# Third attention written out unit by unit, with the products of query tiles two to seven set between its units

## The chip, the cores and the metric

One core of one Trainium2 chip runs the program. The metric is the time of one execution on the device in microseconds (us); of several runs the median counts. Six names are used: PE does the matrix products (PEld is its loading of weights, meaning the stationary operand), DVE, ACT and POOL are the vector, scalar and GpSimd engines, and SP issues most transfers from HBM. Each engine works through its own queue in order, and engines wait for each other on counting semaphores.

## The reference, cut to what matters

The program is a two-block network of 512 tokens and width 1024. Nearly all of it is large products in split precision; the change touches only the last attention, a sliding-window one with sinks, and the projections just before it:

```python
h = rms_norm(x, ln_mix_pre[1])
q, k, v = split(h @ w_in + b_in)          # 16 query heads of 64, 2 key and value heads
s = q . k * 64 ** -0.5                    # blocks of 128 queries against their own and the previous block
s = where(band, s, -inf)
mx = maximum(max(s), sink)
e = exp(s - mx)
p = e / (sum(e) + exp(sink - mx))
o = (p . v) @ w_out + b_out
```

## The kernel before

**Products.** Every 32-bit operand is held as a rounded part and a rest (`_hi`, `_lo`), and `three` (L756 to L765) makes three PE products for each block of 128 rows: hi by hi, lo by hi, hi by lo. A column tile of weights ("chunk") takes eight such steps, 24 products of 512 columns. A chunk arrives as `w_raw` by a transfer of SP, ACT rounds it (`split`, L1449), POOL makes the rest (`rest`, L618), and it stays in a ring of four until PE has used it (`chunks_used`). ACT and POOL work three chunks ahead.

**Projections before the attention.** In this order PE makes the key tile `sk`, the value tile `sv`, query tile `sq0` (in bank 2), the turn of `sv`, and then `sq1` to `sq7`, alternating between banks 0 and 1 of PSUM. For each tile DVE multiplies the bank by the norm (`scaled_by_root`, L2659) and adds bias (`biased`, L2653), ACT rounds its two heads (`round_queries`, L1564), and DVE makes their rests (`rest_of_queries`, L2124). Only then does the attention begin.

**The attention.** There are 64 units, one for each of 16 heads and four blocks of 128 queries; the first block of a head has one block of keys, the others two. A unit passes through these steps: PE makes the scores (`scores`, two products, L967); DVE masks and finds the maximum (`maximum`, L2139); ACT takes the exponential (`exponentials`, L1583); PE turns it (`transposes`, L979); ACT moves the turned tile out of the bank (`move_transposed`, L1598); PE multiplies by the values (`values`, L1008); and after each fourth unit DVE writes a head's output (`output`, L2246). POOL adds the sink's share to the sums (`add_sink`, L668). The order on PE is scores of unit n+5, transposes of n+2, values of n. Scores lie in four banks. PE reads a query head from `q_stage2`, into which POOL copies it (`stage`, L652) ahead of time. Pairs of heads are a loop, with the first pair and the last pairs unrolled.

**Behind it** eight tiles of the output are turned and split (`concat`, `turn_output`, L1055) between the products of the next chunk.

The names on which the steps rest stand in these functions:

## Time and profile before

| | us |
|---|---|
| three runs | 2467.21, 2469.01, 2470.68 (median 2469.01) |
| span of the profiled execution, first to last instruction | 2468.0 |
| PE busy in it | 2423.7 (98%) |
| ACT, POOL, DVE busy | 1079.6, 972.3, 936.0 |
| query tiles one to seven | from 1941.07 to 1979.25 |
| third attention | from 1979.25 to 2039.2 |

The profiled execution has no time of its own apart from its span, which is 1.0 us under the median. A row of the timeline gives start, duration, engine, line, operation, what is written and read, the shapes, and in brackets how long the engine had been idle and who ended that. Durations of PE's products overlap, so that their price is the distance from one start to the next. A window's row gives, for each engine, busy time and number of instructions, then the granted clock of PE (1.00 is 2.4 GHz, 0.50 is 1.2 GHz), the share of the transfer engines and GB/s.

### The profile page before, as it was taken

Reading aid. Unit: us, or ns where it says so; the run is one execution under the profiler, and the core shown is the slowest. Engines: PE = TensorE matmul, PEld = TensorE weight load, DVE = VectorE, ACT = ScalarE, POOL = GpSimd, SP = SyncE. Lnnn points to the kernel's source line nnn. Section 1 sums busy time; section 2 is a strip of 40 time slices with the busy share of each in tenths; the row PEclk is TensorE's granted clock in tenths of the full one; section 3 lists DMA queues with packets and bytes.
Section 4 is the critical chain, followed back from the end, with each engine's and each line's share of the span. In section 5 each row is a group of like instructions: output and inputs, shape, how many; then the busy total and the mean of one; then the engine's idle time right before and its main releaser. Section 6 shows DMA issues by size and latency. Waiting matters only on the chain.

```text
span 2468.0 us, 36248 instructions
## 1 busy us (share of the span) xinstructions
PE 2423.7 (98%) x11990; PEld 2004.0 (81%) x11990; DVE 936.0 (38%) x2051; ACT 1079.6 (44%) x1917; POOL 972.3 (39%) x484
## 2 busy tenths in 40 slices
PE   8999999999999999999999999999999999999998
PEld 6888888888778978888887978788888797788886
DVE  7976322211477753222214243321211773311212
ACT  7565443432347754444335534432332583432321
POOL 4821444444331124444443413444443423444441
PEclk9999999999999999999999999999999999999999
DMA  4300333333420013233332312233333202233331
GB/s 154 116 30 18 90 97 101 94 102 105 128 69 10 1 35 94 93 102 93 103 102 79 103 39 81 77 95 95 100 94 94 69 18 69 86 101 95 94 94 68
DMA packets 57866, 202.75 MB, mean 82 GB/s; under 512 B 7072, under 2 KB 7968, under 8 KB 57392
## 3 DMA queue, kind: packets, MB, share of 16 engines
q1 hardware_dynamic: 54864, 196.02, 26.2%
q10 hardware_dynamic: 2912, 5.55, 0.6%
q8 instruction: 55, 0.90, 0.1%
q14 instruction: 35, 0.29, 0.0%
HBM read 199.44 MB, written 2.10 MB: 82 GB/s over the span
## 4 chain that ended last, share of the span: by engine, by line
PE 41%; issue 14%; POOL 7%; ACT 1%; DVE 1%; POOLq 0%; DVEq 0%; ACTq 0%
PE bank L764 36%; POOL w_lo L618 7%; PE bank L1008 1%; PE bank L967 1%; PE bank L979 1%; ACT h_hi L1492 1%; PE bank L1372 0%; PE bank L1353 0%; ACT gained L1495 0%; PE bank L1367 0%; PE bank L793 0%; PE bank L1055 0%; PE bank L881 0%; PE bank L770 0%; PE bank L786 0%
## 5 line engine op out<-in xcount | busy, mean ns | idle before, releaser
L618 POOL TENSOR_TENSOR w_lo<-w_raw,w_hi 128x1024 fp32r<-128x1024 f32 x368 | 883.3, 2401 | 1197.7 <-ACT w_hi L1449 1188.1
L764 PE MATMUL bank<-h_hi,w_hi 128*128 128x512 f32 x1648 | 650.5, 395 | 7.2 <-DVE tmp L2476 2.1
L764 PE MATMUL bank<-h_lo,w_hi 128*128 128x512 f32 x1648 | 642.2, 390 | 0.0
L764 PE MATMUL bank<-h_hi,w_lo 128*128 128x512 f32 x1648 | 642.2, 390 | 0.0
L1449 ACT ACTIVATE w_hi<-w_raw 128x1024 fp32r<-128x1024 f32 x368 | 386.8, 1051 | 242.7 <-PE bank L764 214.0
L764 PEld LDWEIGHTS bank<-h_hi,w_hi 128*128 128x128 f32 x1648 | 309.8, 188 | 82.3 <-issue 5.9
L764 PEld LDWEIGHTS bank<-h_hi,w_lo 128*128 128x128 f32 x1648 | 309.7, 188 | 65.2
L764 PEld LDWEIGHTS bank<-h_lo,w_hi 128*128 128x128 f32 x1648 | 309.9, 188 | 65.0 <-issue 2.2
L764 PE MATMUL bank<-mact_hi,w_hi 128*128 128x512 f32 x512 | 199.3, 389 | 1.7 <-DVEq L2342 1.7
L764 PE MATMUL bank<-mact_hi,w_lo 128*128 128x512 f32 x512 | 199.2, 389 | 0.0
L764 PE MATMUL bank<-mact_lo,w_hi 128*128 128x512 f32 x512 | 199.2, 389 | 0.0
L764 PE MATMUL bank<-act_hi,w_hi 128*128 128x512 f32 x352 | 136.9, 389 | 0.0
L764 PE MATMUL bank<-act_lo,w_hi 128*128 128x512 f32 x352 | 136.9, 389 | 0.0
L764 PE MATMUL bank<-act_hi,w_lo 128*128 128x512 f32 x352 | 136.9, 389 | 0.0
L1583 ACT ACTIVATE tmp<-bank,nmax 128x128 f32<-128x128 f32 (+2 forms) x240 | 119.1, 496 | 19.7 <-DVE nmax L2139 12.0
L2340 DVE TENSOR_TENSOR tmp<-sq,bank 128x512 f32<-128x512 f32 x64 | 44.0, 688 | 200.2 <-ACT sq L1661 200.2
L1647 ACT ACTIVATE act_hi<-tmp 128x512 f32 x44 | 27.8, 632 | 207.6 <-DVE tmp L2327 207.6
L764 PEld LDWEIGHTS bank<-mact_hi,w_hi 128*128 128x128 f32 x512 | 96.1, 188 | 21.8 <-issue 1.8
L1598 ACT ACTIVATE sq<-bank 128x128 f32<-128x128 f32 (+3 forms) x232 | 92.7, 401 | 48.1 <-PE bank L1008 44.8
L764 PEld LDWEIGHTS bank<-mact_lo,w_hi 128*128 128x128 f32 x512 | 96.1, 188 | 19.9
L764 PEld LDWEIGHTS bank<-mact_hi,w_lo 128*128 128x128 f32 x512 | 96.1, 188 | 19.8
L979 PE MATMUL bank<-ident,tmp 128*128 128x128 f32 x548 | 107.1, 284 | 3.6 <-ACT tmp L1583 1.5
(403 smaller groups left out, 3489.3 us busy)
## 6 DMA issues: line engine op xcount, KB each, us to landing
w_raw<-in_weights SPq DMA_DIRECT2D x368, 512.0 KB, 3.6
out<-x ACTq DMA_DIRECT2D x8, 256.0 KB, 2.1
x<-in_xT SPq DMA_DIRECT2D x4, 256.0 KB, 6.8
x<-in_xT ACTq DMA_DIRECT2D x4, 256.0 KB, 7.4
memx<-in_memT SPq DMA_DIRECT2D x1, 1024.0 KB, 9.8
cmp_w1k<-in_cmp_w ACTq DMA_DIRECT2D x1, 1024.0 KB, 5.6
...
```

What stands on the lines that cost most here:

```text
L618: nc.gpsimd.tensor_tensor(w_lo[:, t % RING, :], w_raw[:, t % RAW, :], w_hi[:, t % RING, :].bitcast(F32), ALU.subtract).then_inc(lo_ready, 1)
L764: r = nc.tensor.matmul(out, a, b, start=first and n == 0, stop=last and n == 2)
L967: r = nc.tensor.matmul(out[:, 0:n], q, k, start=part == 0, stop=part == 1)
L979: r = nc.tensor.transpose(probT_bank[g % 2][:, n * P:(n + 1) * P], prob[:, g % 2, n * P:(n + 1) * P], ident[:, :])
L1008: r = nc.tensor.matmul(output_place(kind, u, g), probT[:, g % 2, n * P:(n + 1) * P], v, start=n == 0, stop=n == len(kts) - 1)
L1449: nc.scalar.activation(w_hi[:, t % RING, :], w_raw[:, t % RAW, :], ACT.Copy).then_inc(hi_ready, 1)
L1492: nc.scalar.activation(h_hi[:, k, :], x_bank(k) if k < BY_PE else x[:, k, :], ACT.Identity, scale=col(name, k)).then_inc(gain_rounded, 1)
L1583: nc.scalar.activation(prob[:, g % 2, 0:n], score_bank[bank_of(kind, u)][:, 0:n], ACT.Exp, bias=nmax[:, s4:s4 + 1], scale=1.0 if kind.star ...
L1598: nc.scalar.activation(probT[:, g % 2, 0:n], probT_bank[g % 2][:, 0:n], ACT.Copy).then_inc(probT_ready[g % 2], 1)
L1647: nc.scalar.activation(act_hi[:, bass.ds(2 * i + f, 1), :].rearrange("p a n -> p (a n)"), tmp[:, f, :], ACT.Copy).then_inc(act_rounded, 1)
L2340: nc.vector.tensor_tensor(tmp[:, f % 2, :], sq[:, f % 2, :], bank[b % 2][:, :], ALU.mult).then_inc(act_made, 1)
```

## The change

- Queries are no longer scaled by 64 ** -0.5; the keys are, once. DVE's bias step for the queries goes: ACT adds the bias while it rounds, and DVE while it makes the rest.
- `q_stage2` and POOL's copies into it go. PE reads `q_swa` itself and waits for `q_split`.
- `sq1` gets bank 3. `sq2` to `sq7` all accumulate in bank 1, one after another. Each is cut into its eight steps of three products: steps 0 to 3 of `sq2` stand before the attention, steps 4 to 7 behind the scores of units 0 to 3, and the 40 steps of `sq3` to `sq7` between transposes and values of units 0 to 39.
- The first step of each of them waits until DVE has moved the tile before it out of bank 1 (`query_moved`). DVE does so at units 0, 8, 16, 24, 32 and 40, behind the maximum of unit n+4 and the output of unit n.
- Scores use three banks (2, 3, 0), and their lead over the values goes from five units to four. The loops are written out.
- POOL makes the rests of the chunks of `sq5` to `sq7` and of the first three chunks of the output projection in four quarters each, behind the sinks of heads 0, 2, 4, 6, 8 and 10. ACT splits those chunks at units 4, 12, 20, 28, 36 and 44, and rounds the queries of tile 2+j at units 8j+1 and 8j+2.

```diff
-OWN["sq0"] = 2
+OWN.update({"sq0": 2, "sq1": 3}, **{f"sq{j}": 1 for j in range(2, KT)})
...
+LOOK_AHEAD = 4
+def swa_unit(n):
+    return (f"swa{n // 32}", 0, n % 8, n % 32 // 8) if n < 64 else None
+def query_step(s):
+    return f"sq{2 + s // KT}", s % KT
+QUERY_STEPS = (KT - 2) * KT
+EARLY_STEPS = 8
...
+    if kind.startswith("swa"):
+        return (32 * int(kind[3]) + 8 * i + u) % 3
...
+            def rest_in_quarters(t):
+                pool.wait_ge(hi_ready, t + 1)
+                for n in range(0, KT * P, 2 * P):
+                    part = slice(n, n + 2 * P)
+                    r = nc.gpsimd.tensor_tensor(w_lo[:, t % RING, part], w_raw[:, t % RAW, part], w_hi[:, t % RING, part].bitcast(F32), ALU.subtract)
+                r.then_inc(lo_ready, 1)
...
+            end = CHUNK["sq1"] + AHEAD + 1
+            rests(start, end)
+            for head in range(2 * SWA_PAIRS):
+                add_sink(*swa_unit(TT * head))
+                if head in (0, 2, 4, 6, 8, 10):
+                    rest_in_quarters(end)
+                    end += 1
+            start = norms(end, ["mlppre1"])
...
+                if kind.startswith("swa") and u % TT == 0:
+                    pe.wait_ge(q_split, 24 + heads_before(kind, u) + 2 * i + 1)
...
-                    pe.wait_ge(probs_ready, g - kind.startswith(("dsa", "mem0", "swa")) + per * i)
+                    pe.wait_ge(probs_ready, g - kind.startswith(("dsa", "mem0")) + per * i)
...
-                    for j in range(1, KT):
-                        column_tile(f"sq{j}")
-                    wait_evacuated(pe, "svT")
-                    pe.wait_ge(first_query_moved, 1)
+                    t = CHUNK["sq1"]
+                    chunk_ready(t)
+                    for k in range(KT):
+                        r = three(of("sq1")[:, :], slot(t, k), (h_hi[:, k, :], h_lo[:, k, :]), k == 0, k == KT - 1)
+                    r.then_inc(chunks_used, 1)
+                    def query_products(s):
+                        name, k = query_step(s)
+                        if k == 0:
+                            chunk_ready(CHUNK[name])
+                            pe.wait_ge(query_moved, int(name[2]) if s else 1)
+                        r = three(of(name)[:, :], slot(CHUNK[name], k), (h_hi[:, k, :], h_lo[:, k, :]), k == 0, k == KT - 1)
+                        if k == KT - 1:
+                            r.then_inc(chunks_used, 1)
+                    for name in ("sk", "sv", "svT"):
+                        wait_evacuated(pe, name)
+                    for s in range(4):
+                        query_products(s)
                     pe.wait_ge(k_split, 13)
-                    def banks_free():
-                        for j in (KT - 2, KT - 1):
-                            wait_evacuated(pe, f"sq{j}")
-                    attention_stream(pe, STREAMS[2], lambda at: attention_begin(at, banks_free), pair_of_heads)
+                    for n in range(4):
+                        if n < 2:
+                            pe.wait_ge(query_moved, n + 1)
+                        scores(*swa_unit(n))
+                        query_products(4 + n)
+                    for n in range(2):
+                        transposes(*swa_unit(n))
+                    for n in range(2 * 4 * SWA_PAIRS):
+                        if swa_unit(n + LOOK_AHEAD):
+                            scores(*swa_unit(n + LOOK_AHEAD))
+                        if swa_unit(n + 2):
+                            transposes(*swa_unit(n + 2))
+                        if EARLY_STEPS + n < QUERY_STEPS:
+                            query_products(EARLY_STEPS + n)
+                        values(*swa_unit(n))
...
+                    def round_query(j, heads=(0, 1)):
+                        act.wait_ge(query_moved, j + 1)
+                        for hh, (part, hi, _) in enumerate(both_heads("swa0", j, sq_q[:, j, :])):
+                            if hh in heads:
+                                bias = col("swa_b_q", j)[HD * hh:HD * hh + HD, :]
+                                nc.scalar.activation(hi, part, ACT.Identity, bias=bias).then_inc(q_rounded, 1)
+                    round_query(0)
+                    split_ahead(CHUNK["sq1"])
+                    round_query(1)
+                    for n in range(LOOK_AHEAD - 1):
+                        exponentials(*swa_unit(n))
+                    for n in range(2):
+                        move_transposed(*swa_unit(n))
+                    for n in range(2 * 4 * SWA_PAIRS):
+                        if swa_unit(n + LOOK_AHEAD - 1):
+                            exponentials(*swa_unit(n + LOOK_AHEAD - 1))
+                        if swa_unit(n + 2):
+                            move_transposed(*swa_unit(n + 2))
+                        done = 2 + n // 8
+                        if n % 8 in (1, 2) and done < KT:
+                            round_query(done, [n % 8 - 1])
+                        if n % 8 == 4 and done < KT:
+                            split_ahead(CHUNK[f"sq{done}"])
...
+                    def move_query(j):
+                        wait_product(dve, f"sq{j}")
+                        nc.vector.tensor_tensor(sq_q[:, j, :], of(f"sq{j}")[:, :], rstd_late[:, :], ALU.mult).then_inc(query_moved, 1)
+                    def rest_of_query(j, heads=(0, 1)):
+                        dve.wait_ge(query_moved, j + 1)
+                        for hh, (part, hi, lo) in enumerate(both_heads("swa0", j, sq_q[:, j, :])):
+                            if hh in heads:
+                                dve.wait_ge(q_rounded, 24 + 2 * j + hh + 1)
+                                bias = col("swa_b_q", j)[HD * hh:HD * hh + HD, :]
+                                nc.vector.scalar_tensor_tensor(lo, part, bias, hi.bitcast(F32), ALU.add, ALU.subtract).then_inc(q_split, 1)
+                    scaled_by_root("sk", sk[:, :])
+                    biased(0, sk[:, :], col("swa_bk"), SCALE)
+                    scaled_by_root("sv", diag[:, :])
+                    biased(1, diag[:, :], col("swa_bv"))
+                    move_query(0)
                     rest_of_both(9, sk[:, :], *k_swa)
-                    last = KT - 1
-                    for j in range(last):
-                        projected(f"sq{j}", j + 2, sq_q[:, j, :], col("swa_b_q", j), SCALE)
-                        if j:
-                            rest_of_queries("swa0", j - 1, sq_q[:, j - 1, :])
-                    scaled_by_root(f"sq{last}", sq_q[:, last, :])
-                    def pair_between_rests(per, at):
-                        for u in range(per):
-                            unit_of_pair(u, at)
-                            if u == 0:
-                                biased(last + 2, sq_q[:, last, :], col("swa_b_q", last), SCALE)
-                            elif u in (1, 2):
-                                rest_of_queries("swa0", last - 1, sq_q[:, last - 1, :], [u - 1])
-                            elif u in (5, 6):
-                                rest_of_queries("swa0", last, sq_q[:, last, :], [u - 5])
-                    attention_stream(dve, STREAMS[2], attention_begin, pair_of_heads, pair_between_rests)
+                    rest_of_query(0)
+                    move_query(1)
+                    hold_sink(0, 0)
+                    for n in range(LOOK_AHEAD):
+                        maximum(*swa_unit(n))
+                    rest_of_query(1)
+                    for n in range(2 * 4 * SWA_PAIRS):
+                        if swa_unit(n + LOOK_AHEAD):
+                            maximum(*swa_unit(n + LOOK_AHEAD))
+                        output(*swa_unit(n))
+                        done = 2 + n // 8
+                        if n % 8 == 0 and done < KT:
+                            move_query(done)
+                        if n % 8 in (2, 3) and done < KT:
+                            rest_of_query(done, [n % 8 - 2])
```

On PE, where the third attention begins, before:

```order
L967 MATMUL bank<-k_swa_hi,q_stage 128x256 [waits probs_ready,evacuated1,evacuated0]
L967 MATMUL bank<-k_swa_lo,q_stage 128x256
L967 MATMUL bank<-k_swa_hi,q_stage 128x256 [waits probs_ready]
L967 MATMUL bank<-k_swa_lo,q_stage 128x256
L770 MATMUL bank<-masks_b,ident_b 128x384 x2
L979 MATMUL bank<-ident,tmp 128x128 [waits probT_ready0,probs_ready]
L967 MATMUL bank<-k_swa_hi,q_stage 128x128 [waits probs_ready,q_staged]
L967 MATMUL bank<-k_swa_lo,q_stage 128x128
L979 MATMUL bank<-ident,tmp 128x128 [waits probT_ready1,probs_ready]
L979 MATMUL bank<-ident,tmp 128x128
```

and in the changed kernel, from the transposes of unit 0 (L1003 are transposes, L991 scores, L783 the products of query tiles, L1032 values):

```order
L1003 MATMUL bank<-ident,tmp 128x128 [waits probT_ready0,probs_ready]
L1003 MATMUL bank<-ident,tmp 128x128 [waits probT_ready1,probs_ready]
L1003 MATMUL bank<-ident,tmp 128x128
L991 MATMUL bank<-k_swa_hi,q_swa 128x128 [waits probs_ready,q_split]
L991 MATMUL bank<-k_swa_lo,q_swa 128x128
L1003 MATMUL bank<-ident,tmp 128x128 [waits probT_ready0,probs_ready]
L1003 MATMUL bank<-ident,tmp 128x128
L783 MATMUL bank<-h_hi,w_hi 128x512 [waits query_moved,lo_ready]
L783 MATMUL bank<-h_lo,w_hi 128x512
L783 MATMUL bank<-h_hi,w_lo 128x512
L1032 MATMUL bank<-sv,sq 128x64 [waits o_done,probT_ready0]
```

The filler products are gone, the query products stand between transposes and values, and the first of them waits for `query_moved`.

On DVE, around the last query tiles of before (L2659 moves a tile, L2653 adds bias, L2124 makes rests, L2139 is the maximum):

```order
L2659 TENSOR_TENSOR sq_q<-bank,spare 128x512 [waits chunks_used]
L2653 TENSOR_SCALAR sq_q<-sq_q,cols 128x512 [waits evacuated0]
L2124 TENSOR_TENSOR q_swa<-sq_q,q_swa 64x512 [waits q_rounded,swa_biased]
L2124 TENSOR_TENSOR q_swa<-sq_q,q_swa 64x512
L2659 TENSOR_TENSOR sq_q<-bank,spare 128x512 [waits chunks_used]
L2143 COPY sink_now<-nsinks 128x1 [waits evacuated1]
L2139 ISA bank,nmax<-bank,masks_b,sink_now 128x128 [waits scores_ready,sink_held]
L2139 ISA nmax 128x1
```

and around unit 8 of the changed kernel, where tile `sq3` is moved (L2304 is the output of a head, L2197 the maximum, L2721 the move):

```order
L2197 ISA bank,nmax<-bank,masks_b,sink_now 128x256 [waits scores_ready]
L2197 ISA nmax 128x1
L2201 COPY sink_now<-nsinks 128x1
L2231 TENSOR_SCALAR sink_shift<-nmax,sinks 128x4 [waits max_ready]
L2304 TENSOR_TENSOR o_tok<-bank,rinv 128x4x64 [waits pv_done,rinv_ready]
L2197 ISA bank,nmax<-bank,masks_b,sink_now 128x128 [waits scores_ready,sink_held]
L2197 ISA nmax 128x1
L2721 TENSOR_TENSOR sq_q<-bank,spare 128x512 [waits chunks_used]
L2197 ISA bank,nmax<-bank,masks_b,sink_now 128x256 [waits scores_ready]
```

The move of a tile used to follow only work on other tiles; now it stands behind a head's output, which waits for `pv_done`, and behind a maximum, which waits for `scores_ready`.

On POOL, in the attention of before (L668 adds the sink, L652 copies a head):

```order
L214 COMPARE_AND_BRANCH
L668 TENSOR_TENSOR oscale<-psum_p,sinkexp 128x4 [waits sink_ready]
L652 COPY q_stage<-q_swa 128x512 [waits q_staged,scores_ready,q_split]
L668 TENSOR_TENSOR oscale<-psum_p,sinkexp 128x4 [waits sink_ready]
L652 COPY q_stage<-q_swa 128x512 [waits q_staged,scores_ready,q_split]
```

and in the changed kernel (L685 adds the sink, L635 is a quarter of a rest, L627 a whole one):

```order
L685 TENSOR_TENSOR oscale<-psum_p,sinkexp 128x4 [waits sink_ready]
L635 TENSOR_TENSOR w_lo<-w_raw,w_hi 128x256 [waits hi_ready]
L635 TENSOR_TENSOR w_lo<-w_raw,w_hi 128x256 x3
L685 TENSOR_TENSOR oscale<-psum_p,sinkexp 128x4 [waits sink_ready] x2
L635 TENSOR_TENSOR w_lo<-w_raw,w_hi 128x256 [waits hi_ready]
```

The copies are gone, and each odd head's sink but the last two now stands behind the rest of a chunk, which waits for `hi_ready`.

## Rows read from the trace of the kernel before

**Rows 1.** Windows: engines' busy time and the granted clock (PEclk) by stage.

```profile
1941.07:1979.25 38.18, 38.18 (x172) 31.63 (x171) 29.82 (x30) 19.11 (x26) 19.60 (x10) 1.00 0.32 98
1979.25:1984.50 5.25, 3.61 (x25) 2.66 (x24) 4.16 (x17) 3.48 (x13) 2.63 (x3) 1.00 0.32 100
1984.50:1991.40 6.90, 6.90 (x36) 6.90 (x35) 4.70 (x16) 5.24 (x19) 0.88 (x3) 0.51 0.00 1
1991.40:2035.00 43.60, 43.55 (x387) 43.24 (x386) 35.59 (x161) 41.46 (x173) 9.83 (x25) 1.00 0.00 1
2039.20:2042.60 3.40, 3.33 (x17) 3.34 (x17) 1.39 (x3) 1.67 (x3) 0.00 (x0) 0.51 0.00 0
```

**Rows 2.** Timeline of PE where the third attention begins; brackets: idle before, and releaser.

```profile
1979.25 0.22 PE L967 MATMUL bank<-k_swa_hi,q_stage 128*128 128x128 f32 x1
...
1980.24 0.35 PE L967 MATMUL bank<-k_swa_hi,q_stage 128*128 128x256 f32 x1 [0.37 <-issue]
...
1980.79 0.50 PE L770 MATMUL bank<-masks_b,ident_b 128*128 128x384 bf16 x2
1981.56 0.33 PE L979 MATMUL bank<-ident,tmp 128*128 128x128 f32 x1 [0.28 <-ACT tmp L1583]
...
1982.33 0.44 PE L979 MATMUL bank<-ident,tmp 128*128 128x128 f32 x2 [0.26 <-ACT tmp L1583]
...
1983.75 0.44 PE L979 MATMUL bank<-ident,tmp 128*128 128x128 f32 x2 [0.73 <-ACT sq L1598]
```

**Rows 3.** Timeline of PE in four units of the settled attention.

```profile
1999.04 0.31 PE L967 MATMUL bank<-k_swa_hi,q_stage 128*128 128x128 f32 x1
...
2000.58 0.36 PE L967 MATMUL bank<-k_swa_hi,q_stage 128*128 128x256 f32 x1
...
2000.90 0.38 PE L979 MATMUL bank<-ident,tmp 128*128 128x128 f32 x2
2001.12 0.56 PE L1008 MATMUL bank<-sv,sq 128*128 128x64 f32 x4
...
2002.28 0.31 PE L967 MATMUL bank<-k_swa_hi,q_stage 128*128 128x128 f32 x1
```

**Rows 4.** Timeline of PE in concat, transposes (L1055) between products (L764).

```profile
2043.70 0.48 PE L764 MATMUL bank<-h_hi,w_hi 128*128 128x512 f32 x1
...
2044.49 0.60 PE L1055 MATMUL bank<-ident,o_tok 128*128 128x128 f32 x4
2044.84 0.48 PE L764 MATMUL bank<-h_hi,w_hi 128*128 128x512 f32 x1
```

**Rows 5.** Timeline of ACT before and at the attention's start.

```profile
1941.94 1.06 ACT L1449 ACTIVATE w_hi<-w_raw 128x1024 fp32r<-128x1024 f32 x1
1942.90 0.58 ACT L1466 ACTIVATE sv<-bank 128x512 f32<-128x512 f32 x1
1948.22 1.29 ACT L1564 ACTIVATE q_swa<-sq_q 64x512 fp32r<-64x512 f32 x2 [4.74 <-DVE sq_q L2653]
...
1978.65 1.28 ACT L1583 ACT_TABLE_LOAD   x1
1981.05 0.37 ACT L1583 ACTIVATE tmp<-bank,nmax 128x128 f32<-128x128 f32 x1 [1.12 <-DVE nmax L2139]
```

**Rows 6.** DVE: one tile's instructions (minimum/median/maximum ns), before the attention.

```profile
L2134 DVE TENSOR_TENSOR k_swa_lo<-sk,k_swa_hi x4: 683/686/2773, 1942.0 to 1946.2; 64x512 fp32r<-64x512 f32 x4
```

**Rows 7.** Timeline of DVE: a tile moved, and a maximum.

```profile
1979.44 0.69 DVE L2659 TENSOR_TENSOR sq_q<-bank,spare 128x512 f32<-128x512 f32 x1 [1.18 <-PE bank L764]
...
1980.51 0.36 DVE L2139 CUSTOM_DVE_ANT_0 bank<-bank,masks_b,sink_now 128x128 f32<-128x128 f32 x1 [0.18 <-DVE sink_now L2143]
```

**Rows 8.** Timeline of DVE: a head's output, in the settled attention.

```profile
2009.99 0.43 DVE L2246 TENSOR_TENSOR o_tok<-bank,rinv 128x256 f32<-128x256 f32 x1
```

**Rows 9.** Timeline of POOL: the rest of a chunk, and a sink.

```profile
1943.08 2.59 POOL L618 TENSOR_TENSOR w_lo<-w_raw,w_hi 128x1024 fp32r<-128x1024 f32 x1 [5.16 <-ACT w_hi L1449]
...
1983.60 0.20 POOL L668 TENSOR_TENSOR oscale<-psum_p,sinkexp 128x4 f32<-128x4 f32 x1 [2.51 <-ACT sinkexp L1589]
```

85 lines of the change are left out of this document (25 added, 60 removed).

## The prediction

> **What bounds the kernel now.** I read the page first: PE is busy 98% of the span, so only what PE executes or waits for counts. Then I read windows over the part that the change touches. From 1941.07 to 1979.25 PE makes query tiles one to seven without a gap: 7 x 24 = 168 products in 38.18 us, 0.227 us each [rows 1]. From 1979.25 to 1984.50 it is busy for only 3.61 of 5.25 us, while it waits for the first exponentials and their copies [rows 1, 2]. Then it is busy all the time but at 1.2 GHz for 6.90 us, and from 1991.40 to 2035 it is busy for 43.55 of 43.60 us at 2.4 GHz [rows 1]. In that settled stretch four units take 1999.04 to 2002.28, that is 3.24 us or 0.81 a unit [rows 3]. ACT is busy for 41.46 of those 43.60 us, so it has 5% to spare and is the next bound there [rows 1]. So there are two things to win: the idle start, and the slow clock behind it. PE is full before and after them, and whatever makes it wait there is new time.
>
> **What goes.** Idle before PE at the start is 0.37 + 0.28 + 0.26 + 0.73 = 1.64 us, and the two filler products add (0.50 - 0.16) = 0.34 [rows 2]: 2.0 us. The slow stretch loses half of 6.9 us, 3.4 us [rows 1]. POOL's copies, DVE's bias steps and the longer scores lead all lie beside PE's work, so removing them is worth nothing in itself. The 168 products and 64 units remain.
>
> **The new start (+1.9).** PE ends `sq1` at about 1946.6 as before and four steps of `sq2` at 1949.3. Meanwhile ACT, no longer held by the roundings, splits the next chunk at once behind the move of `sv` and two roundings: 1943.5 + 1.3 + 1.06 = 1945.9 [rows 5]. POOL's rest of it then runs from 1946.0 to 1948.5 [rows 9]. The fourth rest of the keys would start on DVE at 1946.25, but such an instruction takes 0.69 us alone and took 2.77 us beside a POOL rest, ending with it [rows 6, 9]. So it ends at 1948.7, the two rests of query 0 follow at 0.69 each (taken as those of the keys), and the move of `sq1` ends at 1950.9 [rows 6, 7]. ACT rounds query 1 until 1952.25 (1.29), loads its table until 1953.5 (1.28) and has the first exponential at 1953.9 [rows 5]. The scores of unit 3 need that, since they take the first of only three banks: PE waits 0.25 + 0.5 + 1.0 us before units 0, 1 and 3. Four steps (0.68 each) and the scores (0.25 to 0.32 each) lie between. The second transposes wait 0.45 us more, because exponential 2 needs the buffer of unit 0, which is turned only at 1955.0. Then `sq3` waits for the move of `sq2`, which on DVE stands behind the two rests of query 1 and maximum 4: 1955.3 + 1.4 + 0.4 + 0.7 + 0.14 (below), at 1957.9, where PE is ready at about 1956.3. In all 3.9 us against 2.0: **+1.9**. Bounds: 0, if the start is as idle as now, and +3.
>
> The Trainium skill's page "SBUF — State Buffer", section "Who interferes with whom", says that whichever of DVE and GpSimd comes first holds their shared ports for the whole instruction and the other blocks. The 2.77 us agrees. If the two only shared the port, the start would come out about 1 us better than I have it.
>
> **The clock at the start (-1.7).** Now the clock fell behind a stretch with 1.64 of 5.25 us idle and small products otherwise, and stayed low for 6.9 us [rows 1, 2]. The new start has more idle time from 1953 to 1958, so it should fall again; but behind it come products of 512 columns, and in concat, where such products stand between transposes, the low clock lasted 3.4 us [rows 1, 4]. I take 3.4 us at half speed, which costs 1.7 instead of 3.4: **-1.7**. Ends: -3.4 (it never falls) and 0.
>
> **The wait at each new query tile (+5.8).** `sq4` to `sq7` begin at units 8, 16, 24 and 32, in the bank that the tile before them has just filled. Take the start of the scores of unit n+4 as zero. PE is ready for the new tile after those scores (0.25) and the transposes (0.22), at 0.47. On DVE the move stands behind the output of unit n-1, which waits for the values that PE issued just before zero; in the settled attention that output starts about 0.34 us after the next scores do and takes 0.43 [rows 8]. The maximum of unit n+4 follows: 0.36 us and its small read, until 1.12 [rows 7]. The move takes 0.69, until 1.81 [rows 7], and PE starts 0.14 us after what it waits for (exponential done at 1981.05 + 0.37, transposes at 1981.56) [rows 2, 5]. That is 1.95 - 0.47 = 1.48 us; I take 1.45, and 4 x 1.45 = **+5.8**. Nothing covers it, for PE is in order and the values of unit n stand behind the waiting product. The lower bound has DVE with nothing ahead of the move: 0.69 + 0.14 - 0.47 = 0.36 each, +1.4. The upper one adds 0.25 each, +6.8.
>
> **The switches (+1.0).** In concat three products and four transposes take 2043.70 to 2044.84, 1.14 us [rows 4]. Apart they would be 3 x 0.227 + 4 x 0.11 = 1.12 [rows 1, 3]. 48 such switches at 0.02 make **+1.0**; the bounds are 0 and +3.
>
> **The dense end (+2.7).** From unit 40 there are no query products left, a unit is 0.81 us again and ACT has 5% to spare. Two things fall there. First, ACT rounds query 7 at units 41 and 42 (1.29 us) [rows 5]; about half of it was lead, 0.7 us remains. Second, at unit 44 ACT splits a chunk, POOL makes its rest and only then adds the sink of head 11, for which DVE's output of unit 46 waits; behind that stands maximum 51. Counted from PE's unit 44: ACT's copy done at 1.15, split 2.2, rest 4.7, sink 5.0 [rows 5, 9], then DVE's maximum 5.7 and the exponential 6.4, where PE wants the transposes of unit 51 at 5 x 0.81 + 0.3 = 4.4. That is 2.0 us. Together **+2.7**. Bounds: 0, if the lead of the other engines takes it up, and +4.5, if the scores' shorter lead adds some or the clock falls for 3.4 us behind such a gap. The same chain at units 4 to 36 has PE steps of 0.81 + 0.68 = 1.5 us around it, and the maximum is then in time.
>
> **Sum.** +1.9 - 1.7 + 5.8 + 1.0 + 2.7 = +9.7 us on the span of 2468.0, 2477.7; the median stands 1.0 above that span, so 2478.7.
>
> **Rivals.**
>
> *Not slower: the clock stays whole.* The interleaved products of 512 columns are what PE lacked, so the clock never falls, neither at the start (-3.4) nor in concat, where now 3.4 us are at 1.2 GHz (-1.7) [rows 1], and the dense end finds its engines ahead (0). With start +1.9, tiles +5.8 and switches +1.0 this is +3.6: 2472.6, within 0.2%. For it: the falls follow idle time amid small products. Against: the new start is idler. It needs, at both places, a PE gap of 1 to 2 us leaves the clock alone as long as wide products stand on both sides of it.
>
> *Short waits.* DVE is ahead and only the move itself counts: tiles 4 x 0.36 = 1.4, start +0.5, clock -3.4, switches +1.0, end +0.7: +0.2, 2469.2. With switches at nothing and concat at full clock it is -2.5, and only past that would it be faster by 0.2%. Against: two instructions ahead of the move wait for PE's own latest work.
>
> *The clock falls at every tile.* Each gap of 1.45 us lies beside small products; if it costs 3.4 us at half speed each time, 4 x 1.7, and once more in the dense end, +8.5: 2487.2. Against: half of PE's work around the gaps is wide products, and the clock held through dense small ones [rows 1]. The Trainium skill, page "TensorE: Matmul & The Clock Gate", section "A second HAM failure mode: psum-queue depth-cycling", has a kernel whose short idles between groups of products made the clock swing; it speaks for this case, and no row here shows it.
>
> **Numbers.** The forecast gets 0.50 (own range 2474 to 2483), the whole clock 0.22, short waits 0.13, the clock falling at every tile 0.15. This measurement can tell about 0.2%, 4.9 us, from no change: below 2464.1 or above 2473.9. Faster 0.06 (the far end of short waits), same 0.30, slower 0.64. The range 2468 to 2486 leaves out the far end of short waits and most of the last rival.
>
> **What would show it.** In the timeline of PE: gaps of 1.3 to 1.6 us before the first product of `sq4` to `sq7`, ended by DVE's move, and one of some 1.6 before `sq3`; gaps of 0.5 to 1 us before the scores of units 1 and 3. Per eight units and their 24 products about 8 x 1.5 + 1.45 = 13.5 us. One window at 1.2 GHz near the start. A gap of 1 to 2 us near unit 49, ended by ACT, with POOL's sink late. I am wrong if the gaps at the tiles are under 0.8 us, or if the table load and rounding don't hold the first exponential.

## The result and the profile of the changed kernel

The changed kernel takes 2484.43 us (median of 5 runs, 2482.99 to 2485.73). The kernel before, run beside it, takes 2467.21 (5 runs, 2464.96 to 2470.68). The ratio is 1.0069, 95% interval 1.0057 to 1.0081: slower by 17.2 us. The forecast was 2478.7, in a range of 2468 to 2486: the direction held, and the size came out 5.7 us short.

The profiled execution spans 2481.2 us, 13.2 more than that of before. All of the loss lies in the attention. From the turn of `sv` to the first transposes of concat it takes 1937.78 to 2052.50, 114.7 us; before it took 1940.68 to 2039.27, 98.6. Behind that both need the same 428.7 us. Ahead of it the execution of before was 2.9 us later, since it had two stretches at 1.2 GHz in earlier parts of the program which that of after doesn't have. So +16.1 us are to be explained here, and besides them a granted clock that varies from one execution to the next.

Windows of the changed kernel (PEclk, the granted clock, is 1.00 at 2.4 GHz and 0.50 at 1.2 GHz); columns: stretch, length, busy time of PE, PEld, DVE, ACT and POOL (with counts), granted clock, DMA share, GB/s. They answer to [rows 1].

```profile
1947.00:1956.00 9.00, 5.53 (x28) 3.97 (x29) 6.13 (x18) 5.19 (x14) 0.20 (x1) 1.00 0.14 53
1956.00:1960.30 4.30, 4.30 (x19) 3.88 (x20) 0.55 (x2) 0.97 (x4) 0.00 (x0) 0.60 0.00 0
1960.30:2013.80 53.50, 47.54 (x311) 41.90 (x310) 29.68 (x106) 34.24 (x113) 12.68 (x24) 1.00 0.12 36
2013.80:2018.60 4.80, 4.74 (x20) 4.32 (x21) 0.55 (x2) 1.34 (x5) 0.00 (x0) 0.64 0.12 47
2018.60:2027.00 8.40, 8.40 (x56) 7.43 (x55) 4.86 (x16) 6.49 (x21) 2.81 (x5) 1.00 0.00 0
2027.00:2048.00 21.00, 17.81 (x144) 16.15 (x142) 14.81 (x64) 17.24 (x66) 3.90 (x11) 1.00 0.17 52
```

PE waits in three places: the start (1947 to 1956), the interleaved part (6 us idle of 53.5) and the dense end (2027 to 2048). No other engine is full in any of them: the order of the work makes PE wait, not the speed of another engine. Who ends the waits, over the whole attention (engine, line, waited for: us in total, times, longest):

```profile
PE bank L783 <- DVE sq_q L2721: 7.5, 5, 1.5
PE bank L1003 <- ACT tmp L1630: 3.1, 4, 1.5
PE bank L991 <- ACT tmp L1630: 1.1, 1, 1.1
PE bank L1077 <- DVE o_tok L2304: 0.6, 1, 0.6
PE bank L1003 <- ACT sq L1645: 0.6, 1, 0.6
PE bank L991 <- DVE q_swa L2730: 0.5, 1, 0.5
```

L783 is a query product, L991 the scores, L1003 the transposes, L1077 the first transposes of concat. The first row is the wait for a moved tile, five times 1.5 us.

**The start.** Timeline of PE, its waits (start, duration, what, and in brackets the idle time and its releaser); they answer to [rows 2]:

```profile
1947.09 0.30 PE L991 MATMUL bank<-k_swa_hi,q_swa 128*128 128x128 f32 x1 [0.51 <-DVE q_swa L2730]
1951.67 0.39 PE L991 MATMUL bank<-k_swa_hi,q_swa 128*128 128x256 f32 x1 [1.14 <-ACT tmp L1630]
1953.95 0.41 PE L1003 MATMUL bank<-ident,tmp 128*128 128x128 f32 x2 [0.58 <-ACT sq L1645]
1955.88 0.47 PE L783 MATMUL bank<-h_hi,w_hi 128*128 128x512 f32 x1 [1.51 <-DVE sq_q L2721]
```

One more, 0.15 us before the scores of unit 1 at 1948.39, is too short for the view to list.

**A new tile** (`sq4` here; `sq5` to `sq7` look the same, at 1985.65, 1999.75 and 2013.86). Timeline of POOL, DVE and PE:

```profile
1966.22 2.81 POOL L635 TENSOR_TENSOR w_lo<-w_raw,w_hi 128x256 fp32r<-128x256 f32 x4 [11.31 <-ACT w_hi L1496]
...
1968.99 0.20 POOL L685 TENSOR_TENSOR oscale<-psum_p,sinkexp 128x4 f32<-128x4 f32 x1
...
1969.22 0.18 DVE L2300 RECIPROCAL rinv<-oscale 128x4 f32<-128x4 f32 x1 [1.87 <-POOL oscale L685]
...
1970.11 0.42 DVE L2304 TENSOR_TENSOR o_tok<-bank,rinv 128x256 f32<-128x256 f32 x1
...
1970.44 0.35 DVE L2197 CUSTOM_DVE_ANT_0 bank<-bank,masks_b,sink_now 128x128 f32<-128x128 f32 x1
...
1970.71 0.69 DVE L2721 TENSOR_TENSOR sq_q<-bank,spare 128x512 f32<-128x512 f32 x1
...
1971.54 0.47 PE L783 MATMUL bank<-h_hi,w_hi 128*128 128x512 f32 x1 [1.50 <-DVE sq_q L2721]
```

Read it from the bottom. PE waits for the move; the move stands behind a maximum and a head's output; and ahead of these DVE itself had stood for 1.87 us, since POOL adds the odd head's sink only behind four quarters of a chunk's rest. The prediction had seen the first half of this and not the second.

**The dense end**, at unit 51; timeline of POOL, DVE, ACT and PE:

```profile
2034.59 2.79 POOL L635 TENSOR_TENSOR w_lo<-w_raw,w_hi 128x256 fp32r<-128x256 f32 x4 [5.71 <-ACT w_hi L1496]
...
2037.57 0.18 DVE L2300 RECIPROCAL rinv<-oscale 128x4 f32<-128x4 f32 x1 [2.49 <-POOL oscale L685]
...
2038.32 0.47 ACT L1630 ACTIVATE tmp<-bank,nmax 128x256 f32<-128x256 f32 x1 [1.30 <-DVE nmax L2197]
...
2038.94 0.33 PE L1003 MATMUL bank<-ident,tmp 128*128 128x128 f32 x1 [1.47 <-ACT tmp L1630]
```

**The ledger** of the attention, after less before:

| part | read from | us |
|---|---|---|
| start | 3.9 us of waits against 2.0 (1.64 of waits and 0.34 of filler products) | +1.9 |
| four new tiles | 4 x 1.50 | +6.0 |
| interleaving | 40 units, 74.4 us from the scores of unit 4 to those of unit 44, less 8.1 idle and 3.4 for two slow stretches, leaves 62.9; the parts alone are 40 x (0.811 + 3 x 0.2273) = 59.7 | +3.2 |
| dense end | scores of unit 44 to those of unit 60: 17.69 against four times 3.24 | +4.7 |
| clock | two stretches of 3.41 us at half speed, against one of 6.83, each taken at half its length | 0 |
| sum | against 16.1 measured | +15.8 |

Half the length is an estimate, and the rows don't bear it out. The eight units with a tile wait take 14.10 us at full clock (7.81 + 6.29) and 15.67 where the second slow stretch lies (9.35 + 6.32); the first one cost 1.5 us too (units 4 to 8 take 10.11, and 8.56 in experiment one with the same waits and full clock). The stretch of 6.83 us before cost 2.1 (experiment eleven). By these prices the clock's row is +1.0, the interleaving's +3.5, and the ledger comes to 17.1: 1 us too much instead of 0.3 too little.

### The profile page after: what moved, and what is told of

Same layout as the page of the kernel before. It is cut to its first block and busy times, and to the rows that moved or that the text cites. A ratio compares the mean times of both kernels' runs of the same rounds, so it can differ in the third digit from the quotient of the medians.

```text
span 2481.2 us, 35897 instructions
## 1 busy us (share of the span) xinstructions
PE 2425.2 (98%) x11988; PEld 2001.8 (81%) x11988; DVE 926.3 (37%) x2043; ACT 1080.4 (44%) x1917; POOL 963.8 (39%) x486
## 5 line engine op out<-in xcount | busy, mean ns | idle before, releaser
L627 POOL TENSOR_TENSOR w_lo<-w_raw,w_hi 128x1024 fp32r<-128x1024 f32 x362 | 868.5, 2400 | 1178.3 <-ACT w_hi L1496 1168.7
L783 PE MATMUL bank<-h_hi,w_hi 128*128 128x512 f32 x1648 | 654.4, 397 | 14.9 <-DVE sq_q L2721 7.5
L783 PE MATMUL bank<-h_hi,w_lo 128*128 128x512 f32 x1648 | 643.0, 390 | 0.0
L783 PE MATMUL bank<-h_lo,w_hi 128*128 128x512 f32 x1648 | 642.8, 390 | 0.0
L783 PEld LDWEIGHTS bank<-h_hi,w_hi 128*128 128x128 f32 x1648 | 310.2, 188 | 88.9 <-issue 14.4
L783 PEld LDWEIGHTS bank<-h_hi,w_lo 128*128 128x128 f32 x1648 | 309.7, 188 | 65.4
L783 PEld LDWEIGHTS bank<-h_lo,w_hi 128*128 128x128 f32 x1648 | 310.1, 188 | 62.9 <-issue 2.2
L783 PE MATMUL bank<-mact_hi,w_hi 128*128 128x512 f32 x512 | 199.5, 390 | 1.7 <-DVEq L2398 1.7
L783 PE MATMUL bank<-mact_hi,w_lo 128*128 128x512 f32 x512 | 199.4, 389 | 0.0
L783 PE MATMUL bank<-mact_lo,w_hi 128*128 128x512 f32 x512 | 199.3, 389 | 0.0
L783 PE MATMUL bank<-act_hi,w_lo 128*128 128x512 f32 x352 | 137.1, 389 | 0.0
L783 PE MATMUL bank<-act_lo,w_hi 128*128 128x512 f32 x352 | 137.0, 389 | 0.0
L783 PE MATMUL bank<-act_hi,w_hi 128*128 128x512 f32 x352 | 137.0, 389 | 0.0
L1630 ACT ACTIVATE tmp<-bank,nmax 128x128 f32<-128x128 f32 (+2 forms) x240 | 118.8, 495 | 17.1 <-DVE nmax L2197 11.6
L783 PEld LDWEIGHTS bank<-mact_hi,w_hi 128*128 128x128 f32 x512 | 96.1, 188 | 21.7 <-issue 1.8
L1003 PE MATMUL bank<-ident,tmp 128*128 128x128 f32 x548 | 107.4, 285 | 6.2 <-ACT tmp L1630 4.1
L783 PEld LDWEIGHTS bank<-mact_hi,w_lo 128*128 128x128 f32 x512 | 96.1, 188 | 19.9
L783 PEld LDWEIGHTS bank<-mact_lo,w_hi 128*128 128x128 f32 x512 | 96.1, 188 | 19.8
## 6 DMA issues: line engine op xcount, KB each, us to landing
memx<-in_memT SPq DMA_DIRECT2D x1, 1024.0 KB, 10.1
```

The source lines that it names most:

```text
L627: nc.gpsimd.tensor_tensor(w_lo[:, t % RING, :], w_raw[:, t % RAW, :], w_hi[:, t % RING, :].bitcast(F32), ALU.subtract).then_inc(lo_ready, 1)
L783: r = nc.tensor.matmul(out, a, b, start=first and n == 0, stop=last and n == 2)
L1003: r = nc.tensor.transpose(probT_bank[g % 2][:, n * P:(n + 1) * P], prob[:, g % 2, n * P:(n + 1) * P], ident[:, :])
L1630: nc.scalar.activation(prob[:, g % 2, 0:n], score_bank[bank_of(kind, u, i)][:, 0:n], ACT.Exp, bias=nmax[:, s4:s4 + 1], scale=1.0 if kind.s ...
```

## The experiments

Every kernel ran five or more times beside the kernel before. Experiments one to four shared a chip, five to eight another, nine to eleven a third; the kernel before took 2467.16, 2468.53 and 2466.97 us there, so times from two groups compare to some 1.5 us. An interval of a ratio is about 3 us wide to either side for five runs and 2.2 for eleven. "Both" below is the name of experiment three's kernel. All timelines and waits are of one execution each.

**One: POOL's rests behind the odd head's sink.**

```diff
-                if head in (0, 2, 4, 6, 8, 10):
+                if head in (1, 3, 5, 7, 9, 11):
                     rest_in_quarters(end)
```

> The changed kernel, but POOL makes the rest of each chunk behind the sink of the odd head, no longer ahead of it. Theory (POOL's quarters hold the odd head's sink, that holds DVE's reciprocal, and DVE everything behind it): the gap of 1.47 us at unit 51 goes, and each of the four tile gaps of 1.50 us falls to about 1.1, since DVE then waits only for PE's own values ahead of the move; 1.4 + 4 x 0.4 = 3.0 us less, about 2481.4 us. Rival (the held reciprocal is only one of several late steps, and PE's own latest values bind the tile gaps): gaps at the tiles stay at 1.4 to 1.5, only unit 51 gains, 1.4 us less, about 2483.0. Second rival (the chunk's rest is then late, or the split of ACT ahead of it was what held unit 51): no change, 2484.4.

Measured: 2479.58 us, ratio to before 1.0049 (1.0036 to 1.0063). That is 4.9 less than the changed kernel, where 3.0 were expected. The trace has the mechanism as expected: DVE's reciprocal no longer waits, unit 51's gap is gone (scores of 44 to 60 take 16.30 instead of 17.69), and the gap before a new tile is

```profile
1970.87 0.42 DVE L2304 TENSOR_TENSOR o_tok<-bank,rinv 128x256 f32<-128x256 f32 x1 [0.45 <-PE bank L1032]
1971.22 0.35 DVE L2197 CUSTOM_DVE_ANT_0 bank<-bank,masks_b,sink_now 128x128 f32<-128x128 f32 x1
...
1971.48 0.68 DVE L2721 TENSOR_TENSOR sq_q<-bank,spare 128x512 f32<-128x512 f32 x1
...
1972.31 0.47 PE L783 MATMUL bank<-h_hi,w_hi 128*128 128x512 f32 x1 [1.11 <-DVE sq_q L2721]
```

Now the output waits 0.45 us for PE's own values, as the prediction had drawn it. So the predicted chain is worth 1.11 us, and POOL's sink the other 0.4 of the 1.50. The other 1.9 us of the gain aren't gaps; at equal granted clock (0.996, 0.997, 0.998; one or two runs each of experiment one) it takes 3.7, 4.2 and 5.3 less than the changed kernel.

**Two: a tile is moved as soon as it is full.** On DVE the move stands ahead of the output of units 7, 15, 23 and 31, and that of `sq2` ahead of the rests of query 1.

```diff
-                    rest_of_query(1)
+                    move_query(2)
+                    rest_of_query(1)
...
+                        if n % 8 == 7 and 3 + n // 8 < KT:
+                            move_query(3 + n // 8)
                         output(*swa_unit(n))
                         done = 2 + n // 8
-                        if n % 8 == 0 and done < KT:
-                            move_query(done)
```

> The changed kernel, but DVE moves a finished query tile as soon as its last product is out: the moves of tiles three to six stand ahead of the output of units 7, 15, 23 and 31 instead of behind that of units 8, 16, 24 and 32, the move of tile two ahead of the rests of query 1. Theory (order on DVE sets the gap before each new tile): each of four gaps falls from 1.50 to about 0.6 us, not to nothing, because POOL's sink still holds DVE ahead of it, and the wait before sq3 from 1.51 to about 0.2; 4 x 0.9 + 1.3 = 4.9 us less, about 2479.5 us. Rival (DVE is held by POOL for so long that its order doesn't matter): the gaps stay above 1.2 us, at most 1 us less plus the 1.3 of the start, about 2482. Unit 51's gap of 1.47 us stays by both.

Measured: 2479.30 us, ratio 1.0050 (1.0036 to 1.0063), 5.1 less. The waits for a tile, the changed kernel's 7.5 us in five:

```profile
PE bank L783 <- DVE sq_q L2721: 3.6, 4, 0.9
```

The one before `sq3` is gone, the others are 0.90 and not 0.6: still POOL, which holds DVE's reciprocal for 1.88 us ahead of the move. The gap at unit 51, expected to stay at 1.47, is 0.90; in this execution a slow stretch (2029.16 to 2032.57) lies just ahead of it and makes PE come later.

**Three: both edits.**

> The changed kernel with both edits: POOL's rests behind the odd head's sink, DVE's moves ahead of the outputs. Theory: the four tile gaps fall to 0.1 to 0.3 us (4 x 1.3 = 5.2 less), the wait before sq3 to about 0.2 (1.3 less), unit 51's gap goes (1.4 less): 7.9 us less, 2476.5 us; if the stretch of 3.41 us at 1.2 GHz behind the fourth tile gap was set off by that gap, it goes too, another 1.7 less, 2474.8. Rival (the edits take away one late step each and the next is as late): the two gains don't add, 4 to 5 us less than the changed kernel, about 2480. That it comes below the kernel before (2467.2) is expected by neither, since the interleaved stretch itself still takes 6.3 us per four units where its parts need 5.97.

Measured: 2471.77 us (11 runs), ratio 1.0019 (1.0010 to 1.0028), 12.7 less than the changed kernel. It beat the lower of the expected numbers by 3. No product waits for a tile any more. The waits in its attention, without the turn of `sv`:

```profile
PE bank L1003 <- ACT tmp L1630: 1.6, 3, 0.6
PE bank L991 <- ACT tmp L1630: 1.2, 1, 1.2
PE bank L1077 <- DVE o_tok L2304: 0.6, 1, 0.6
PE bank L991 <- DVE q_swa L2730: 0.6, 1, 0.6
PE bank L1003 <- ACT sq L1645: 0.6, 1, 0.6
PE bank L1003 <- DVE o_tok L2304: 0.4, 1, 0.4
```

The gaps that went are 6.0 + 1.5 + 1.4 = 8.9 us. In PE's waits the edits gain more together (8.8) than apart (2.9 + 4.9 = 7.8): with either alone, the other still holds DVE. The medians say the same (12.7 against 4.9 + 5.1 = 10.0), but by less than their intervals. Of the two attentions, 114.7 and 102.4 us, the 3.4 us that the gaps don't explain go with the two slow stretches, which the profile of the changed kernel has in this part and that of both hasn't. That belongs to the two executions and only in part to the kernels: at equal granted clock both is 10.1 (0.997) and 11.2 us (0.998) faster than the changed kernel, not 12.7, and 1 to 2 us of it stay unexplained.

**Four: the lead alone, in the kernel before.**

```diff
-    return 5 if kind.startswith("swa") else 4
+    return 4
```

> The kernel before, with its scores in the third attention four units ahead instead of five, the four banks and the query staging as they are. Theory (it is the shorter lead that made four units at the changed kernel's end take 3.64 us instead of 3.24): 16 groups of four units at 0.4 more, 6.4 us more at most, about 2473 us, with gaps before the transposes ended by ACT. Rival (the lead doesn't matter where a fourth bank lets the scores go at once; it was the third bank's wait that made it): no change, 2467.2, and the 3.24 us for four units stay.

Measured: 2473.42 us, ratio 1.0025 (1.0015 to 1.0036): 6.3 more than before. Timeline of PE in a settled stretch, four units from 2008.36 to 2012.00, 3.64 us against the 3.24 of [rows 3]:

```profile
2009.01 0.36 PE L967 MATMUL bank<-k_swa_hi,q_stage 128*128 128x256 f32 x1
2009.21 0.28 PE L967 MATMUL bank<-k_swa_lo,q_stage 128*128 128x256 f32 x1
2009.54 0.44 PE L979 MATMUL bank<-ident,tmp 128*128 128x128 f32 x2
2009.82 0.56 PE L1008 MATMUL bank<-sv,sq 128*128 128x64 f32 x4
```

The transposes start 0.33 us behind the second product of the scores where they need 0.12: the exponential that they turn is late, by too little to look like a gap. That is the changed kernel's 3.64 at its end, and the fourth bank didn't help: the lead, not the bank, costs it. (The expected gaps ended by ACT show at 0.2 to 0.9 us in the first twenty units and near the end; in the settled part they are below what the view lists.)

**Five: products ahead of the transposes** (on top of both).

```diff
+                        if EARLY_STEPS + n < QUERY_STEPS:
+                            query_products(EARLY_STEPS + n)
                         if swa_unit(n + 2):
                             transposes(*swa_unit(n + 2))
-                        if EARLY_STEPS + n < QUERY_STEPS:
-                            query_products(EARLY_STEPS + n)
```

> As the kernel both (rests behind the odd head's sink, moves ahead of outputs), but in the loop the step's three query products stand between the scores and the transposes, instead of behind the transposes. In both, the second product of a step begins 0.31 us after the first where such products follow each other every 0.227, and four interleaved units take 6.30 us where their parts need 5.97. Theory (a fixed price of 0.085 us where wide products follow small instructions, whatever these are): it stays 6.30 us for four units, the time stays within 1 us of both's, 2471.8. Rival (the price belongs to products behind transposes): the 0.31 becomes 0.23, 40 x 0.085 = 3.4 us less, 2468.4. In either case PE comes to each new tile 0.22 us sooner, which could open gaps there again, at most 4 x 0.2.

Measured: 2470.67 us, ratio 1.0019 (1.0010 to 1.0028), not to be told from both by time. The timelines of PE tell more. Both, products behind transposes:

```profile
1992.89 0.38 PE L1003 MATMUL bank<-ident,tmp 128*128 128x128 f32 x2
1993.03 0.48 PE L783 MATMUL bank<-h_hi,w_hi 128*128 128x512 f32 x1
1993.34 0.40 PE L783 MATMUL bank<-h_lo,w_hi 128*128 128x512 f32 x1
1993.58 0.39 PE L783 MATMUL bank<-h_hi,w_lo 128*128 128x512 f32 x1
```

Products behind scores:

```profile
1986.82 0.28 PE L991 MATMUL bank<-k_swa_lo,q_swa 128*128 128x256 f32 x1
1986.94 0.40 PE L783 MATMUL bank<-h_hi,w_hi 128*128 128x512 f32 x1
1987.17 0.39 PE L783 MATMUL bank<-h_lo,w_hi 128*128 128x512 f32 x1
1987.40 0.39 PE L783 MATMUL bank<-h_hi,w_lo 128*128 128x512 f32 x1
```

From the first product to the second it is 0.31 us behind transposes and 0.23 behind scores of 256 columns (0.28 where they have 128). Four units fall from 6.30 to 6.04, near the 5.97 of their parts. So the price belongs to transposes right ahead of wide products: the rival was right. But PE now comes to each new tile sooner, waits 0.21 us for it (0.54 before `sq3`), and the second product is slow again behind that wait, so eight units take 12.48 instead of 12.61 and five times that is a gain of 0.6 us.

**Six: two steps behind every even unit, none at the odd ones** (on top of both).

```diff
-                        if EARLY_STEPS + n < QUERY_STEPS:
-                            query_products(EARLY_STEPS + n)
+                        for s in (n, n + 1):
+                            if n % 2 == 0 and EARLY_STEPS + s < QUERY_STEPS:
+                                query_products(EARLY_STEPS + s)
```

> As the kernel both, but two steps of query products behind the transposes of every even unit and none at the odd ones, so 20 places where products and small work alternate in the loop instead of 40. Theory (0.085 us for each alternation, paid on PE itself): 20 x 0.085 = 1.7 us less, 2470.1, and four units at 6.13 us where no gap is. Rival (the alternation costs nothing as such and the products only cover late exponentials; the odd units then run bare and wait for ACT): gaps ended by ACT before the transposes of the units without products, 2 to 6 us more than both, 2474 to 2478.

Measured: 2484.18 us, ratio 1.0070 (1.0056 to 1.0083): 12.4 more than both, twice the most that the rival gave. In eight units (1974.41 to 1988.99) PE waits

```profile
PE bank L1003 <- ACT tmp L1631: 1.3, 2, 0.6
PE bank L783 <- DVE sq_q L2722: 0.7, 1, 0.7
```

and without these 1.9 us they take 12.65 against 12.61. So halving the alternations saved next to nothing that can be read here. One step a unit is what the interleaving lives on: each step covers the 0.6 us by which the next exponential would be late.

**Seven: query 1 rounded in the loop** (on top of both), on ACT and DVE behind unit 0.

```diff
-                    round_query(1)
                     for n in range(LOOK_AHEAD - 1):
                         exponentials(*swa_unit(n))
...
+                        if n == 0:
+                            round_query(1)
```

> As the kernel both, but query 1, which is not read before unit 8, is rounded on ACT behind unit 0's work in the loop instead of ahead of the first exponential, and its rests on DVE likewise. Theory (ACT's two roundings, 1.29 us, hold the first exponential): the waits of 1.15 and 0.58 us before the scores of unit 3 and the second transposes fall to 0.2 and 0.3, the 0.59 before unit 1 stays; 1.2 us less, 2470.6. Rival (the first exponential is then held by ACT's table load and DVE's first maxima, which are as late): less than 0.3 us, 2471.6.

Measured: 2472.80 us, ratio 1.0020 (1.0010 to 1.0030), no gain in time. The wait of 1.15 us is gone, and a new one stands in the loop, so that the first eight units take 12.0 us against 12.6:

```profile
1953.43 0.41 PE L1003 MATMUL bank<-ident,tmp 128*128 128x128 f32 x2 [0.58 <-ACT sq L1645]
1957.08 0.33 PE L1003 MATMUL bank<-ident,tmp 128*128 128x128 f32 x1 [0.47 <-ACT tmp L1630]
```

Half a microsecond of the expected 1.2 was given back at once, as ACT still has to do the roundings while PE is short of exponentials.

**Eight: four banks and the lead of five from unit 48** (on top of both). The query tiles' bank is free by then.

```diff
-        return (32 * int(kind[3]) + 8 * i + u) % 3
+        n = 32 * int(kind[3]) + 8 * i + u
+        return n % 3 if n < 48 else (n - 49) % 4
...
+def ahead_of(n, lead):
+    return [n + lead] if n < 43 else [n + lead, n + lead + 1] if n == 43 else [n + lead + 1]
```

> As the kernel both, but from unit 48 the scores use four banks, the query tiles' bank among them, and run five units ahead, with the exponentials four. Theory (the lead of four in three banks costs 0.4 us per four units in the dense end, as a lead of four cost the kernel before 6.3 us over 64 units): the last four groups of four fall from 3.64 to 3.25 us, 1.6 us less, 2470.2, and the first of them gives back 0 to 0.3 for the scores that are issued twice in one unit. Rival (it is ACT's own load, not the lead, that sets 3.64): no change, 2471.8.

Measured: 2471.36 us, ratio 1.0014 (1.0005 to 1.0023). The last two groups of four units fall from 3.68 and 3.64 to 3.27 and 3.25, and the attention is 1.35 us shorter than in both (101.1 against 102.4). The median shows only 0.4 of it, less than such a measurement can tell.

**Nine: all five edits.**

> The changed kernel with all five edits: rests behind the odd head's sink, moves ahead of outputs, products ahead of transposes, query 1 rounded in the loop, four banks from unit 48. From the attention sections of the profiles so far (both 102.4 us, products ahead of transposes 0.7 less, later rounding 0.7 less, four banks 1.35 less) the gains should add, since they fall in different places: 2.75 us less than both, about 2469, no less than the kernel before. Rival (the edits of the start shift the same ACT work into the same gap): 1.5 us less, 2470.3. Neither expects it below 2467.

Measured: 2468.61 us (12 runs, 2465.67 to 2471.35 but for one of 9325.24, of which no cause is on record), ratio 1.0003 (0.9994 to 1.0012): not to be told from the kernel before. At equal granted clock (0.997, 0.998, 0.999; the table is in experiment eleven) it is 2.0, 1.6 and 1.7 us slower. The attention takes 99.0 us, 3.4 less than in both, where the profiles one by one had promised 2.75.

**Ten: only tile seven is spread.** `sq2` to `sq6` are made ahead of the attention in two banks by turns; the attention is written out, without staging, and goes to four banks and the lead of five at unit 12.

```diff
-OWN.update({"sq0": 2, "sq1": 3}, **{f"sq{j}": 1 for j in range(2, KT)})
+OWN.update({"sq0": 2, "sq1": 3}, **{f"sq{j}": j % 2 for j in range(2, KT)})
...
+                    for j in range(2, KT - 1):
+                        t = CHUNK[f"sq{j}"]
+                        chunk_ready(t)
+                        pe.wait_ge(query_moved, j - 1)
...
-                        if EARLY_STEPS + n < QUERY_STEPS:
-                            query_products(EARLY_STEPS + n)
```

> The written-out attention without staging, but query tiles two to six are made ahead of it as in the kernel before, in two banks by turns, and only tile seven is spread: four steps ahead of the first scores, one behind each of the scores of units 0 to 2, one behind the first two transposes. From unit 12 the scores use four banks and run five units ahead. Theory (the switches, the lead of four and the tile gaps are what the changed kernel pays, and wide products are what the kernel before lacks at its start): start waits under 1 us against 2.0, switches 0.4 at most, from unit 8 on 3.25 to 3.3 us per four units, and no stretch at 1.2 GHz in the attention, which costs the kernel before 3.4 us at its start: 3.5 to 5 us less than the kernel before, 2462 to 2464. Rival (the clock falls all the same, since small work follows): 0 to 1.5 us less than before, 2466 to 2468. Second rival (ACT, with 5% to spare, gives back both roundings of tile seven and the later start as gaps in the dense part): 2468 to 2471.

Measured: 2466.82 us, ratio 0.9997 (0.9988 to 1.0007): 17.6 less than the changed kernel, and by its median no faster than the one before. At equal granted clock it is 0.6 (0.997, seven runs), 1.0 (one) and 2.0 us (0.999, two) faster. No wait is left at the start; in the dense part PE is held by

```profile
PE bank L1007 <- ACT sq L1659: 0.9, 2, 0.6
PE bank L995 <- ACT tmp L1644: 0.7, 2, 0.4
```

From unit 36 on four units take 3.25 us; four groups ahead of that take 3.6 to 4.0. They lie where the lead changes and where tile seven is rounded, which is the second rival's mechanism, though the time lies in the first rival's range. The first rival's mechanism isn't in this profile: from 1977.60 to 2037.00 the granted clock is 1.00. No experiment separates what the slow groups owe to the lead and to the rounding.

**Eleven: the kernel before with its start filled.**

```diff
-                filler({"dsa": 0, "nsa0": 3, "swa0": 2}[at(0)[0]], o_bank[1])
+                filler({"dsa": 0, "nsa0": 3, "swa0": 3}[at(0)[0]], o_bank[1])
...
+                    if swa:
+                        filler(1 + 2 * u, o_bank[1])
```

> The kernel before with five more filler products (bf16, 384 columns, 0.17 us each, written to a bank that nobody reads) at its attention's start: one ahead of the first transposes, one between them and three behind them, in the places where PE waits. They fill 0.9 of the 1.64 us of idle time and should not delay anything. Theory (the stretch of 6.9 us at 1.2 GHz comes from that idle time): it goes, 3.4 us less, 2463.8. Rival (the clock falls by how the small products of the attention lie, whatever the idle time): the stretch stays, no change within 0.5, 2467.5.

Measured: 2467.47 us, ratio 1.0005 (0.9996 to 1.0014). The profile shows the start at full clock,

```profile
1983.00:1990.00 7.00, 6.76 (x58) 6.39 (x57) 6.58 (x26) 6.64 (x26) 1.27 (x3) 1.00 0.03 8
```

against 0.51 in the third of [rows 1], and yet nothing was won, at equal granted clock neither (0.2 us less at 0.997, 1.0 more at 0.999). Two things account for it. Up to the scores of unit 20 the filled kernel takes 17.67 us and the one before 19.80: the slow stretch cost 2.1, not 3.4. DVE and ACT are nearly full where the clock is whole (6.58 and 6.64 of 7.00), so they probably use the slow stretch to catch up; that is argued, not shown. And the stretch isn't there in every execution. That the fillers drove it away isn't shown either: experiment four has no fillers added, waits more at its start (0.38 + 0.27 + 0.44 + 0.41 + 0.85 us), and has the full clock there too (1.00 from 1977 to 1990). The 74 runs of the kernel before that stood beside these experiments, by the mean granted clock of each:

| granted clock | runs | median us |
|---|---|---|
| 0.999, 1.000 | 29 | 2464.8 |
| 0.998 | 8 | 2466.8 |
| 0.997 | 14 | 2468.3 |
| 0.996 | 7 | 2469.5 |
| 0.995 | 16 | 2471.4 |

One stretch of 3.41 us at half speed takes 0.0007 off a span's mean clock. A run at 0.999 has room for one beside the end of the span, which is slow in every profile (1.6 to 2.7 us in eleven of thirteen, 5 to 6 in the others), so at least the 29 of the first line didn't have the profile's 6.83 us at the attention's start. The table also gives the price: 0.001 of mean clock, 4.9 us at half speed, goes with 1.6 us, a third of the length, as 2.1 is of 6.83. The profile that the prediction used had a clock of 0.996, one of the slower executions, and its slow stretches aren't in every execution of the same code. Their places aren't arbitrary, though. The thirteen profiles (one of each kernel here) have a slow stretch at the start of concat in six, near 95 us in six, near 227 in five, and near 745 and 895 in four. The Trainium skill, page "TensorE: Matmul & The Clock Gate", section "What's actually happening", calls the number of slow matmuls at a kernel's start variable from run to run; these runs agree, in the middle of a program too.

## Why the prediction was right, and where it wasn't

**The start, +1.9: right in sum and place.** 3.9 us of waits were forecast (the terms add up to 3.8) and 3.9 came: before units 0, 1 and 3, the second transposes and `sq3` they were 0.5, 0.15, 1.1, 0.6 and 1.5, against 0.25, 0.5, 1.0, 0.45 and 1.6. The blocked rests of the keys came as forecast as well: beside a POOL rest two of the four took 2.78 us, the other two 0.69. Only they don't end with POOL's rest, as the prediction read the row, but 0.55 us behind it (1943.25 and 1946.06 against 1942.70 and 1945.51; before, 1946.22 against 1945.67).

**The new tiles, +5.8: the size came out (4 x 1.50), the mechanism only in part.** The working gave 1.48 us from DVE's output and maximum ahead of the move. Experiment one shows this chain to be worth 1.11: output and maximum took 0.61 us from start to start of the move, where I had allowed 0.78, and PE was ready 0.2 later than I took it. The missing 0.4 was POOL's: the sink behind the quarters. The rival of short waits, 0.36 us a tile, is out. I had used this very chain for unit 51 and dismissed it for units 4 to 36, with the words that the maximum is then in time. It was, but the output and the move behind it weren't. That is the step of the working that failed, and two errors cancelled.

**The switches, +1.0: mis-sized, +3.2.** I took 0.02 us each from one place in concat. Over 40 units it was 0.08: 0.31 from the first product to the second instead of 0.23, less 0.04 by which the first starts early, 0.02 where the transposes come late behind the scores (0.137 against 0.118 us, in both), and the rest in hundredths at the other steps. My upper bound of 3 was just too low.

**The dense end, +2.7: the mechanism as forecast, the size +4.7.** The gap at unit 51 was given 2.0 and took 1.47. What I had left to the bound ("if the scores' shorter lead adds some") was the larger part: 0.4 us for each of four groups, shown by experiment four. A row that was there pointed to it: ACT had 5% to spare [rows 1], and a lead shorter by a unit takes 0.81 us out of the chain from scores to transposes. The remaining 1.5 us stand before the transposes of units 45, 46 and 48, against 0.7 forecast. The first two (0.51 + 0.43) come right behind ACT's roundings of tile seven (0.71 and 0.72 us, at 2029.77 and 2031.12; the view puts the second wait down to DVE's output, but ACT's exponential ended at 2032.33, 0.15 before the transposes), the third (0.58) behind its split of a chunk (1.05 us at 2033.46), which the forecast charged to unit 51 alone. No experiment took these away, so the link is argued only.

**The clock, -1.7: wrong, and more than the number.** I priced the slow stretch of one profile as the kernel's own. Profile against profile the term came out at 0 by half the lengths and at +1.0 by what the stretches cost: the changed kernel had 3.41 us near the start, as forecast, and 3.41 more behind the fourth tile. At equal granted clock the two kernels differ by 15.1 (0.996, three runs of the changed one), 16.2 and 16.2 us (0.997 and 0.998, one run each). None of the changed kernel's five runs reached 0.999, where 29 of 74 of before did; that probably makes up the last us to 17.2. Whether a gap of 1.5 us sets off a fall stayed open. One of the four tile gaps was followed by a slow stretch in the profile, so the rival in which all are was wrong, and so was, for this execution, the one in which the clock stays whole; but experiment one has the same waits at its start (3.8 us) and the full clock, and both is the one profile with no slow stretch but the last 2.4 us of its span. What sets off a slow stretch isn't known from these runs.

**The sum.** The terms without the clock were +11.4 and became 15.8; of these 4.4 us the switches hold 2.2 and the dense end 2.0. The clock, at 0, adds 1.7. Together that is 6.1, and the median fell 5.7 us beyond the forecast. That the two agree so well is in part luck: the 1.0 us from span to median isn't a constant of the kernel (runs of the kernel before take 2.2 us more than their spans, so that the profiled execution took about 2470.2 and was slower than the median), and the changed kernel's spans grew by less than its attention, 13.2 against 16.1 us. Two terms came out beyond their own bounds (switches 3.2 of 3, dense end 4.7 of 4.5); the time stayed within the range, 1.6 us from its end, because start and tiles came out as given.
